# Sixteen routed experts: tiles of 32 rows side by side in plain float32, in place of slots of 128 rows in split float32

## The reference

```python
def hier_moe(u, w_gr, b_gr, w_er, b_er, w1, w3, w2):
    ...
    gsel = jnp.argmax(gl, axis=-1)
    ...
    vals, ids = lax.top_k(el_sel, EXPERT_TOPK)
    ...
    def expert_block(args):
        xb, gb = args
        a = jnp.einsum('td,edf->tef', xb, w1)
        b = jnp.einsum('td,edf->tef', xb, w3)
        hid = jax.nn.silu(a) * b * gb[:, :, None]
        return jnp.einsum('tef,efd->td', hid, w2)
```

## Time and profile before

| | us |
|---|---|
| three runs | 728.72, 726.08, 728.53 (median 728.53) |
| profiled execution, its own time | 726.84 |
| profiled execution, its span | 725.5 |
| outside the span | 1.34 |
| expert stage in the span, first `up` matmul to last `down` matmul | 301.28 to 477.71 |

### The profile page before, as it was taken

How to read it: one execution, slowest core, us unless ns; L and a number is a source line. 1 busy time by engine, 2 the same in 40 slices (tenths; PEclk the granted TensorE clock), 3 DMA queues, 4 the chain that set the end, 5 groups by cost and what they waited for, 6 DMA issues and landing times.

```text
span 725.5 us, 9902 instructions
## 1 busy us (share of the span) xinstructions
PE 701.7 (97%) x3750; PEld 564.6 (78%) x3750; DVE 514.3 (71%) x757; ACT 378.6 (52%) x542; POOL 64.1 (9%) x74
## 2 busy tenths in 40 slices
PE   4999999999999999899999999989999999999997
PEld 2887676777888877788877777769888888888886
DVE  1456898537587774885558998887998675766854
ACT  3334425645536344564447877738624548744442
POOL 0002110331020000000000000011002502300000
PEclk9999999999999999999999999999999999999999
DMA  9999688589346931756579999945444575545531
GB/s 287 348 280 385 246 299 320 203 298 340 117 149 228 348 113 59 253 184 191 186 243 338 366 365 357 379 155 174 146 136 126 164 218 171 171 149 193 166 135 59
DMA packets 104894, 164.01 MB, mean 226 GB/s; under 512 B 10896, under 2 KB 53741, under 8 KB 104718
## 3 DMA queue, kind: packets, MB, share of 16 engines
q1 hardware_dynamic: 102942, 155.47, 64.6%
q0 software_dynamic: 1904, 7.90, 3.1%
HBM read 162.26 MB, written 1.08 MB: 225 GB/s over the span
## 4 chain that ended last, share of the span: by engine, by line
PE 84%; DVE 7%; DMA 3%; ACT 2%; SPq 2%; issue 1%; POOL 1%; ACTq 0%; DVEq 0%; POOLq 0%
PE p L577 24%; PE p L579 23%; PE p L578 23%; PE p L646 2%; DMA s_raw<-in_w_in_dram 2%; PE p L1229 2%; PE p L635 2%; DVE s_rawr L1847 2%; PE p L692 1%; POOL s_L L518 1%; ACT s_hi L1399 1%; DMA s_raw<-in_w_exp_up_dram 1%; PE p L704 1%; DVE s_PP L1958 1%; PE p L1108 1%
## 5 line engine op out<-in xcount | busy, mean ns | idle before, releaser
L1847 DVE TENSOR_TENSOR s_rawr<-s_raw,s_hi 128x1024 fp32r<-128x1024 f32 x240 | 290.7, 1237 | 49.5 <-ACT s_hi L1399 48.6
L1399 ACT ACTIVATE s_hi<-s_raw 128x1024 fp32r<-128x1024 f32 x240 | 246.6, 1055 | 132.1 <-PE p L579 61.6
L577 PE MATMUL p<-s_hi,s_Ah 128*128 128x512 f32 (+1 forms) x384 | 154.0, 401 | 0.6 <-DVE s_Al L1866 0.3
L579 PE MATMUL p<-s_hi,s_Al 128*128 128x512 f32 (+1 forms) x384 | 148.2, 386 | 0.0
L578 PE MATMUL p<-s_rawr,s_Ah 128*128 128x512 f32 (+1 forms) x384 | 148.1, 386 | 0.0
L577 PE MATMUL p<-s_hi,s_Bh 128*128 128x512 f32 x256 | 101.9, 398 | 2.9 <-DVE s_rawr L1847 2.7
L579 PE MATMUL p<-s_hi,s_Bl 128*128 128x512 f32 x256 | 100.0, 390 | 0.0
L578 PE MATMUL p<-s_rawr,s_Bh 128*128 128x512 f32 x256 | 99.8, 390 | 0.0
L577 PEld LDWEIGHTS p<-s_hi,s_Ah 128*128 128x128 f32 x384 | 72.1, 188 | 26.3 <-issue 7.2
L579 PEld LDWEIGHTS p<-s_hi,s_Al 128*128 128x128 f32 x384 | 72.1, 188 | 15.1
L578 PEld LDWEIGHTS p<-s_rawr,s_Ah 128*128 128x128 f32 x384 | 72.3, 188 | 12.7
(11 more groups left out here) (379 smaller groups left out, 818.7 us busy)
## 6 DMA issues: line engine op xcount, KB each, us to landing
s_raw<-in_w_in_dram SPq DMA_DIRECT2D x80, 512.0 KB, 4.9
s_raw<-in_w_exp_gate_dram SPq DMA_DIRECT2D x64, 256.0 KB, 4.3
s_raw<-in_w_exp_up_dram SPq DMA_DIRECT2D x64, 256.0 KB, 5.6
s_raw<-in_w_exp_down_dram SPq DMA_DIRECT2D x32, 512.0 KB, 5.9
s_GS<-in_w_ada_dram SPq DMA_DIRECT2D x12, 1024.0 KB, 7.2
s_raw<-in_w_gate_dram SPq DMA_DIRECT2D x16, 512.0 KB, 9.9
s_GS<-in_w_ada_dram SPq DMA_DIRECT2D x8, 512.0 KB, 8.9
s_raw<-in_w_ret_out_dram SPq DMA_DIRECT2D x8, 512.0 KB, 3.5
```

The lines of the kernel that those rows point to most:

```text
L577: pe.matmul(o, xh, wh, start=start, stop=False)
L579: return pe.matmul(o, xl, wh, start=False, stop=stop)
L1399: act.activation(T.hi[:, i % NHL, :], T.raw[:, i % NRAW, :], ACT.Copy).then_inc(*S.hi(i))
L1847: dve.tensor_tensor(T.lo[:, i % NRAW, :], T.raw[:, i % NRAW, :], T.hi[:, i % NHL, :].bitcast(F32), ALU.subtract).then_inc(*S.lo_dve(i))
```

## The change

The experts' weights leave the list of pieces. They come in 24 units of 2.1 MB, in three buffers of `s_WX` (which lies over the slots of `s_raw` and `s_hi`). A unit holds one quarter of `up` or one half of `down` of expert e of each of the four groups, for e = 0 to 3. No register is in the source address, and SP may load a unit without waiting for the router. Each row's place is now in one of 11 tiles of 32 rows. Tile t < 4 holds the first 32 rows of group t, so its weights are at a fixed place in the unit. Tiles 4 to 10 hold the overflow of the groups, and the group of each is known at run time only: DVE (`put`, L2435) copies the weights of tiles 4 to 7, ACT (L1743) those of 8 to 10, from an offset in a register to a fixed place (`s_put`, `s_ZC`, `s_RGS`). PE multiplies in three rounds for each half unit (`tiles`, L1157): tiles 0 to 3 from `s_WX`, 4 to 7, 8 to 10. Numbers are plain float32: nothing is split for the experts.

```diff
+UNITS = [("up", 0, h) for h in range(4)]
+for e in range(2):
+    UNITS += [("up", e + 1, 0), ("down", e, 0), ("down", e, 1)] + [("up", e + 1, h) for h in (1, 2, 3)]
+UNITS += [("up", 3, h) for h in range(4)] + [("down", e, c) for e in (2, 3) for c in range(2)]
...
+TILES = ((0, 1, 2, 3), (4, 5, 6, 7), (8, 9, 10))
+ROWS_OF = (128, 128, 96)
...
+def raw_free(S, i):
+    first = AT["bq", 0]
+    if first <= i < first + NRAW:
+        return unit_done(S, LAST - 2 + i % NRAW // 4)
+    return piece_done(S, i - NRAW)
...
+    def unit(v, gs):
+        for g in gs:
+            if v >= 3:
+                q.wait_ge(*unit_done(S, v - 3))
+            else:
+                w = 4 * v + g
+                q.wait_ge(*piece_done(S, max(i for i in range(AT["pl", 0] + 2) if (i % NRAW == w if w < NRAW else i % NHL == w - NRAW))))
+            for dst, src in unit_parts(I, v, g, T.WX[:, 4 * (v % 3) + g, :]):
+                sp.dma_start(dst, src).then_inc(*S.unit_in[v % 3](v))
...
+    unit(0, range(4))
+    unit(1, (0, 1))
+    unit(2, (2, 3))
     q.wait_ge(*S.dve_res.at("x", 1, 1))
     sp.dma_start(T.G1[:, :], I["masks"]).then_inc(*S.masks_in(0))
...
-    q.wait_ge(*S.dve_route.at("order"))
-    for j in range(4):
-        base.append(sp.value_load(T.gi[0:1, j:j + 1], min_val=0, max_val=12))
-        pieces((AT[f"up{4 * j + 4}", 0] if j < 3 else len(PIECES)) - done[0])
+    unit(1, (2, 3))
+    unit(2, (0, 1))
+    for v in range(3, LAST + 1):
+        unit(v, range(4))
+    pieces(len(PIECES) - done[0])
...
+    def tiles(v, j, s, x, o, start, stop):
+        for n, t in enumerate(TILES[s]):
+            w = T.WX[:, 4 * (v % 3) + t, 512 * j:512 * j + 512] if s == 0 else T.put[j][t - 4]
+            r = pe.matmul(o[32 * n:32 * n + 32, :], x[:, 32 * t:32 * t + 32], w, start=start, stop=stop, tile_position=(0, 32 * n))
+        r.then_inc(*S.round(v, j, s))
...
     def put(v, j):                                     # ACT; DVE's is like it, for tiles 4 to 7
+        q.wait_ge(*unit_landed(S, v))
+        q.wait_ge(*(S.round.at(v - 1, j, 2) if v else S.pe_gather.at(0)))
+        for t in (4, 5, 6):
+            act.activation(T.put[j][t], put_source(T, v, j, of[t - 4]), ACT.Copy).then_inc(*S.act_put(v, j))
```

More of the change, by code:

```diff
@@ L85, in piece_list @@
     some("pl", range(2))
[L86 to L90, removed]
     for name in SECOND:
@@ L335, in signals @@
     S.slots_in = land("slots")
+    S.unit_in = [land(f"unit{b}") for b in range(3)]
     S.piece, S.turned, S.ada = of("pe_piece"), of("pe_turned"), of("pe_ada")
@@ L1103, in hidden_cols @@
[L1103 to L1106, removed]
-            for k in range(2):
[L1108 to L1125, removed]
+    gather(0, S.dve_route.at("logits"))
@@ new lines, in weights_there, with up_half @@
+    def weights_there(v, j, s):
+        q.wait_ge(*(unit_landed(S, v), S.dve_put.at(v, j), S.act_put.at(v, j))[s])
+    def up_half(e, h, j):
+        v = UAT["up", e, h]
+        for s in range(3):
+            weights_there(v, j, s)
+            if e == 0:
+                q.wait_ge(*gathered(2 * h + j))
+            if h == 0 and j == 0:
+                if e:
+                    q.wait_ge(*S.dve_moe.at("hid", e - 1, s))
+                else:
+                    q.wait_ge(*gathered((4, 1, 7)[s]))
+            tiles(v, j, s, T.XG[:, 2 * h + j, :], T.U[s], h == 0 and j == 0, h == 3 and j == 1)
@@ new lines, in down_half @@
+    def down_half(e, c, j):
+        v = UAT["down", e, c]
+        for s in range(3):
+            weights_there(v, j, s)
+            if s == 2:
+                q.wait_ge(*S.dve_moe.at("ht", e))
+                if j == 0 and (e or c):
+                    q.wait_ge(*S.dve_moe.at("y2", e - 1 + c, 1 - c))
+            else:
+                q.wait_ge(*S.act_moe.at("ht", e))
+            tiles(v, j, s, T.HT[:, e % 2, j, :], down_bank(T, s, c), j == 0 and (e == 0 or s == 2), j == 1 and (e == 3 or s == 2))
@@ L1138, in pe_program @@
[L1138 to L1150, removed]
@@ L1151, in pe_program @@
-    q.wait_ge(*S.dve_route.at("by slot"))
[L1152 to L1166, removed]
-        down(n, 0, (0, 1), (f"dn{n}", 0, 1))
-        down(n, 1, (0, 1), (f"dn{n}", 1, 1))
@@ new lines, in pe_program @@
+    q.wait_ge(*S.dve_route.at("back"))
+    q.wait_ge(*S.dve_route.at("own gates"))
+    for s in range(3):
+        for tt in range(2):
+            r = pe.matmul(T.turn3[0:ROWS_OF[s], 4 * s:4 * s + 4], T.P[:, tt, 128 * s:128 * s + ROWS_OF[s]].bitcast(F32), T.own[:, tt, :], start=tt == 0, stop=tt == 1)
+    r.then_inc(*S.pe_route("gates"))
+    up(0, 3)
+    q.wait_ge(*S.dve_route.at("by slot"))
+    for e in range(3):
+        up_half(e + 1, 0, 0)
+        turn_two(e)
+        up_half(e + 1, 0, 1)
+        turn_last(e)
+        if e < 2:
+            down(e, 0)
+            down(e, 1)
+        for h in (1, 2, 3):
+            up(e + 1, h)
@@ L1179, in pe_program @@
+    down_half(2, 0, 0)
+    turn_two(3)
+    down_half(2, 0, 1)
+    turn_last(3)
+    down(2, 1)
+    down(3, 0)
+    down(3, 1)
+    q.wait_ge(*S.act_moe.at("ht", 3))
+    q.wait_ge(*S.dve_moe.at("ht", 3))
+    for s in range(3):
+        rows_back(s, 0)
+    q.wait_ge(*S.dve_moe.at("y2", 3, 1))
+    for s in range(3):
+        rows_back(s, 1)
     m_free[0] = m_free[1] = S.dve_moe.at("gy", 1, 1)
@@ new lines, in act_program @@
+    full(1), full(3)
+    put(0, 0)
+    full(5), full(7)
+    put(0, 1)
+    for v in range(1, LAST + 1):
+        put(v, 0)
+        kind, e, h = UNITS[v - 1]
+        if (kind, h) == ("up", 3):
+            silu(e)
+        if v == 1:
+            q.wait_ge(*S.dve_route.at("ev"))
+            act.activation(ev, ev, ACT.Exp).then_inc(*S.act_route("ev"))
+        if v == LAST:
+            rows_out(0, 0), rows_out(1, 0)
+        put(v, 1)
+        if (kind, h) == ("up", 3):
+            hid_cols(e)
+        if v == LAST:
+            rows_out(2, 0)
@@ L2375, in dve_program, with put @@
+    def put(v, j):
+        q.wait_ge(*unit_landed(S, v))
+        if v or j:
+            q.wait_ge(*(S.round.at(v - 1, j, 1) if v else S.pe_gather.at(7)))
+        else:
+            q.wait_ge(*S.piece.at("wo1", 3, 1))
+        for t in range(4):
+            dve.tensor_copy(T.put[j][t], put_source(T, v, j, of[t])).then_inc(*S.dve_put(v, j))
+    put(0, 0)
+    full(0), full(2), full(4), full(6)
+    put(0, 1)
+    put(1, 0)
     q.wait_ge(*S.act_route.at("ge"))
```

467 lines of the change are left out of this document (228 added, 239 removed).

## The result

The changed kernel takes **697.74 us** (median of 4 runs, 697.25 to 701.28), the kernel before 727.39 us beside it: a ratio of 0.9603, interval [0.9563, 0.9642]. The forecast was 687.5 us. The sign is right, the range holds the time, and the time is 10.2 us above the forecast. The profiled execution took 698.22 us, 28.6 us less than the 726.84 us of the one before.

What follows compares the result with a forecast made beforehand. TensorE bounds the kernel; after the change bytes pace the expert stage, whose last `down` ends at 431.0 against 477.71. Minus 46.7, plus 6.5 given back, is 40.2 us less: 686.6 profiled, 688.3 for a median, forecast 687.5 us, range 677 to 707.

Steps and rivals of the forecast that it cites:

- What bounds the kernel: Whole kernel: TensorE limits; in the expert stage, once its work is much smaller, 50.3 MB of weights remain, 137 us.
- What a round costs: Expert matmuls on TensorE: 0.44 us a round at the fast clock, 2.6 us a unit, 63 us for 24 units.
- The unit's own path and the cover: Expert stage, from a unit's landing to its last round: about 4 us, below 5.71, so transfers run without a gap.
- the cost of a change of expert: Between experts: SiLU, gate and transposes, about 3 us for every six units, covered by the two units in hand.
- What transfers and copies cost: Per unit of the expert stage: transfer 5.71 us, ACT's copies 3.1 us, DVE's 2.8 us; register addresses cost nothing.
- A window from 315 to 425: Sign in the expert stage that bytes set the pace: DMA share over 1.0 and about 365 GB/s throughout.
- Rival D: Expert stage: ACT's copies with register addresses cost 1.3 us each, 7.8 us a unit, kernel slower at 745; chance 0.06.
- The start: Before and into the expert stage: 4 MB fetched early under the router's work, unit 0 ending at 303.5 to 304.
- Rival C: Expert stage: bytes pace it but DVE's gates hold units 1 to 3, a late start, 697; chance 0.04.
- What is given back: Behind the last `down`: later first sum +3.5 us, `bq` +1.8, clock +1.2, sum +6.5 us.
- the 1.2 us for it: Behind the expert stage: allowance of 1.2 us for TensorE's granted clock falling to 0.50 with a thinner stage ahead.
- Rival B: Expert stage: TensorE stays at half clock, 5.3 us a unit, 5.95 to 6.5 with waits, 705 to 713; chance 0.15.

Runs made afterwards that it cites:

- light rounds: The changed kernel with every matmul of the experts' rounds taking 128 of its 512 columns, copies and transfers kept: 690.03 us, ratio 0.9486 to the kernel before the change.
- after: The kernel with the whole change, against the kernel before it: 697.74 us, ratio 0.9603.

## Why the forecast was right in kind and 10 us low

**What bounds the kernel.** Right: with TensorE's work in the stage made smaller, the bytes come up as a limit. The kernel with a quarter of the columns takes 2.5 us more than the forecast. Part of that nearness is luck: its last round ends 4.4 us later than forecast, and less is given back behind it than I had put down.

**What a round costs: this term was mis-sized.** I took the 16 records of the earlier trace rows for 16 matmuls in four rounds and divided 1.92 - 0.59 by three: 0.44 us. They are 8 matmuls in two rounds, two records each, and 0.44 us is the distance between the records of one matmul. A round costs 0.86 us at full clock and a unit 5.15 us, not 2.6. All 24 units are 124 us of TensorE, not 63, so the work fell from 166 us by a quarter and not by more than half. The check was to be had before: in that window the program calls 16 matmuls on `s_GS,s_CS` (four weight blocks of four), and the group counts 32. The other row, eight records in 1.94 us, is one round at the slow level.

**The unit's own path and the cover: failed, as a consequence.** I wrote that transfers run without a gap, since a buffer would be free 6 us before the queue is empty. With 5.15 us of rounds TensorE has no reserve, and any delay on one side starts one on the other: a late transfer holds SiLU back (2.6 us), the rounds behind it hold a buffer longer, SP waits for them, and the next transfer has a gap. The stage takes 146.1 / 24 = 6.1 us a unit, above both TensorE's own 5.5 and the 5.8 of the bytes. That this is the cause is shown: either side made light ends the stage at 433 or 435, and freeing buffers early, which removes no work at all, gives back 5 us, with SiLU moved and the gate split 7. I had put the cost of a change of expert at nothing, under the two units in hand; the waits for `s_hid` were 8.0 us, 1.28 us of them a table load that I had not counted.

**Size.** The last `down` ended 15.3 us later than forecast. The kernel with rounds of 0.45 us ends at 435.4, so 10.9 us of it go with the price of a round. With light rounds unit 3 is fetched at 303.12, so its fetch at 305.63 in after (forecast 304) belongs to the price of a round too. The other 4.4 us lie in the transfers: with light rounds the copies of the last unit wait for its landing until 430.14 (forecast 425.4), 127.0 us behind the fetch of unit 3, where I had 121.4. Of these 5.6 us the rates explain 1.3: 13 up units at 6.0 us cost 3.8 us more than at 5.71, 8 down units at 5.4 us 2.5 us less. What the rest is stays open. 15.3 less 3.7 us (6.5 - 2.8, below) is the distance of the profiled 698.22 to the forecast's own 686.6; for the medians 0.9 us that I had added and 0.5 us between profile and median come off, which leaves 10.2.

**What transfers and copies cost.** Up units 6.0 us, down units 5.4 us, around the 5.71 taken. A window from 315 to 425 was to show about 365 GB/s at a share over 1.0 and shows 335 at 1.00. ACT's copies are 1.67 us for three, so 0.52 us apart, DVE's 1.43 us for four, 0.34 apart (0.35 taken). So a register in the address shows no cost: 0.52 us is what ACT's copies of the earlier trace rows took without one. Rival D is gone.

**The start.** Right: the first round starts at 300.23, and the early 4 MB matter by 5 us. Rival C's late start did not happen; that the time is near its price of 697 is chance.

**What is given back: too much.** From the last `down` to `bq` it is 455.22 - 446.3 = 8.9 us instead of 6.5, +2.4, and in the whole 31.4 us of stage became 28.6 us of time: 2.8 given back where I had 6.5. DVE's first sum starts 449.31 - 446.3 = 3.0 us behind the last round, 1.7 us before the change: +1.3 where I had +3.5.

```profile
449.31 0.42 DVE L2540 TENSOR_TENSOR s_ZC<-s_YR,p 128x256 f32<-128x256 f32 x1 [0.48 <-PE p L1221]
```

From there to `bq` it is 5.9 us in place of 4.8: +1.1 where I had +1.8. The clock did not fall behind the stage (granted clock 1.00 from 446 to 458 us), so the 1.2 us for it were not needed. In the kernel with light rounds it was at 0.50 from 435.4 to 439.0, and `bq` came some 2 us later behind its last round than here.

**Rival B.** Its price was closer than its cause. It gave 5.3 us a unit and 5.95 to 6.5 with the waits, and 6.1 was measured, but at a granted clock of 0.99. The clock fell once, to 0.81, 0.50 and 0.84 in the windows of 2 us from 398 on, around the 2.65 us wait that ends at 399.64; around the waits of 2.77 and 2.62 us it stayed at 1.00. In the kernel with light rounds B's cause is there, 0.59 over the stage. The Trainium skill, "TensorE: Matmul & The Clock Gate", HAM oscillation, says that bursts between waits for DMA run at half clock again and again. This case agrees where TensorE was busy 78 of 135 us and not where it was busy 134 of 146.

## What to carry to other kernels

Before a record's distance is read as the price of an instruction, count the program's instructions against the group's count; a plain float32 matmul left two here. When two limits come out as near each other as here (stages of 133 and 135 us), the stage can cost more than the larger one (146 us), and then the question is what holds the buffers and what stands behind a late transfer in each engine's queue. Free a buffer at its last reader, not at the end of the unit, and put work that does not need the next transfer ahead of the work that does.

## What was not expected of the hardware

- A plain float32 matmul of 128x32x512 takes 0.86 us, and four of them in the four column tiles take 0.86 us together.
- Reading 2 KB from every 8 KB of HBM instead of rows of 1 KB in a line costs the whole kernel 33 us (730.5 against 697.7), with packets of 1 KB and of 2 KB alike. From 344 to 350 us, at a share near 1, it was 248 GB/s with packets of 1 KB and 290 with 2 KB, against 350 in full stretches of after.
- Rounds made four times shorter brought the granted clock from 0.99 to 0.59 in the stage, so that a quarter of the columns took half the time.
